# Moving the normed activations 64 bytes down in on-chip memory, in a five-layer fp32 transformer kernel

## The reference

```
h = layer_norm(ALPHA * h + mix, ln_g[i, 0], ln_b[i, 0])
h = layer_norm(ALPHA * h + square(relu(h @ w1)) @ w2, ln_g[i, 1], ln_b[i, 1])
```

```
x = x + 0.5 * (silu(n(x) @ w1) * (n(x) @ w3)) @ w2      # n: rmsnorm with a gain
x = x + hybrid_mixer(n(x), ...)
x = x + 0.5 * (silu(n(x) @ w1) * (n(x) @ w3)) @ w2
return n(x)
```

## Time and profile before

| | before |
|---|---|
| time, median of 3 runs | 2042.54 us (2042.12 to 2045.98) |
| time of the profiled execution | 2042.28 us |
| span of the profiled execution, first to last instruction | 2040.5 us |
| TensorE matmul busy | 1995.2 us, 98% of the span |
| TensorE weight loads busy | 1764.5 us, 86% |
| VectorE busy | 1321.0 us, 65% |
| ScalarE busy | 918.5 us, 45% |
| mean granted TensorE clock | 0.999 of full |

### The profile page before, as it was taken

One profiled execution on the slowest core, in us unless ns is written; L12 is line 12 of the kernel. 1 busy time (PEld: TensorE's weight loads), 2 busy tenths in 40 slices (PEclk: granted clock), 3 DMA queues, 4 the chain that ended last, 5 costly groups with the idle time before them and its releaser, 6 DMA issues.

```text
span 2040.5 us, 28917 instructions
## 1 busy us (share of the span) xinstructions
PE 1995.2 (98%) x12302; PEld 1764.5 (86%) x12302; DVE 1321.0 (65%) x1312; ACT 918.5 (45%) x860; POOL 22.5 (1%) x45
## 2 busy tenths in 40 slices
PE   8999999999999999999999999999999999999998
PEld 7988888797888888888988888889998997998997
DVE  6665866798756768667756666674445446666444
ACT  5345333367343554333344443443335445644444
POOL 0000000000000000000000000000000000000000
PEclk9999999999999999999999999999999999999999
DMA  8444555545545434555535455535556553344442
GB/s 335 167 158 173 186 181 189 186 150 186 217 175 206 143 147 186 189 185 185 204 124 206 160 202 205 179 121 188 188 201 218 168 142 124 124 165 155 185 185 103
DMA packets 31989, 361.72 MB, mean 177 GB/s; under 512 B 3805, under 2 KB 4066, under 8 KB 9746
## 3 DMA queue, kind: packets, MB, share of 16 engines
q1 hardware_dynamic: 28146, 347.49, 46.1%
q0 software_dynamic: 3744, 12.77, 2.6%
HBM read 359.15 MB, written 1.10 MB: 177 GB/s over the span
## 4 chain that ended last, share of the span: by engine, by line
PE 86%; DVE 8%; ACT 4%; issue 1%; DMA 0%; SPq 0%; DVEq 0%; ACTq 0%
PE acc L935 25%; PE bank L1541 9%; PE bank L825 8%; PE bank L827 8%; PE bank L826 7%; PE bank L1543 4%; DVE w_lo L2528 2%; PE bank L1554 1%; PE bank L864 1%; PE acc L947 1%; PE bank L866 1%; PE bank L865 1%; ACT w_hi L1938 1%; PE bank L1170 1%; PE bank L1658 1%
## 5 line engine op out<-in xcount | busy, mean ns | idle before, releaser
L2533 DVE TENSOR_TENSOR w_lo<-raw,w_hi 128x4096 fp32r<-128x4096 f32 (+4 forms) x83 | 310.2, 3737 | 117.3 <-ACT w_hi L1949 117.3
L825 PE MATMUL bank<-ht_both,w_hi 128*128 128x256 f32 x1344 | 376.8, 280 | 0.3 <-DVE oa_lo L3134 0.3
L827 PE MATMUL bank<-ht_both,w_lo 128*128 128x256 f32 x1344 | 375.5, 279 | 0.0
L826 PE MATMUL bank<-ht_both,w_hi 128*128 128x256 f32 x1344 | 375.0, 279 | 0.0
L1938 ACT ACTIVATE w_hi<-raw 128x2048 fp32r<-128x2048 f32 x166 | 309.6, 1910 | 136.2 <-PE bank L827 117.9
L1949 ACT ACTIVATE w_hi<-raw 128x4096 fp32r<-128x4096 f32 (+4 forms) x91 | 283.5, 3116 | 178.6 <-PE bank L1543 156.7
L2528 DVE TENSOR_TENSOR w_lo<-raw,w_hi 128x2048 fp32r<-128x2048 f32 x98 | 220.0, 2287 | 88.5 <-ACT w_hi L1938 88.5
L1541 PE MATMUL bank<-ht_both,w_hi 128*128 128x512 f32 x768 | 269.1, 393 | 0.0
L825 PEld LDWEIGHTS bank<-ht_both,w_hi 128*128 128x128 f32 x1344 | 251.9, 187 | 3.2 <-issue 1.3
L826 PEld LDWEIGHTS bank<-ht_both,w_hi 128*128 128x128 f32 x1344 | 252.3, 188 | 1.5 <-issue 0.5
L827 PEld LDWEIGHTS bank<-ht_both,w_lo 128*128 128x128 f32 x1344 | 252.2, 188 | 0.0
(11 more groups left out here) (470 smaller groups left out, 3355.5 us busy)
## 6 DMA issues: line engine op xcount, KB each, us to landing
raw<-slabs_in SPq DMA_DIRECT2D x147, 2048.0 KB, 7.8
raw<-slabs_in SPq DMA_DIRECT2D x23, 1024.0 KB, 6.9
raw<-slabs_in SPq DMA_DIRECT2D x12, 512.0 KB, 11.0
g_tab<-gains_in POOLq DMA_DIRECT2D x11, 512.0 KB, 4.4
b_tab<-gains_in POOLq DMA_DIRECT2D x8, 512.0 KB, 5.1
raw<-slabs_in SPq DMA_DIRECT2D x2, 1152.0 KB, 5.7
raw<-slabs_in SPq DMA_DIRECT2D x1, 1280.0 KB, 6.0
a_bias<-bias_rows POOLq DMA_DIRECT2D x8, 128.5 KB, 3.4
```

The source lines that it names most:

```text
L825: nc.tensor.matmul(o, whi, xhi, start=first, stop=False)
L826: nc.tensor.matmul(o, whi, xlo, start=False, stop=False)
L827: return nc.tensor.matmul(o, wlo, xhi, start=False, stop=last)
L2533: nc.vector.tensor_tensor(w_lo[ring][:, 0:w], raw[ring][:, 0:w], w_hi[slot][:, 0:w].bitcast(F32), ALU.subtract).then_inc(lo_ready, 1)
```

## The change

`ht_both` starts 64 bytes lower, at the weight slots' own remainder (0 instead of 64), and the bytes left free stand behind it, so that `cst` and all that follows stay where they were. The list of instructions is the same on every engine, in the same order and with the same waits; only the start addresses within `ht_both` differ.

```
         h = sb("h", [P, TT, D])
-        off_w(64)
         ht_both = sb("ht_both", [P, KD, 2, S], F32R)
         ht_hi = ht_both[:, :, 0, :]
         ht_lo = ht_both[:, :, 1, :]
-        off_w(192)
+        off_w(256)
         cst = sb("cst", [P, C_KEEP])
```

## The result

| | before | changed |
|---|---|---|
| median in the comparison | 2044.26 us (4 runs) | 2054.39 us (4 runs) |
| ratio to before | | 1.0050, 95% interval 1.0037 to 1.0062 |
| profiled execution | 2042.28 us | 2054.16 us |
| its span | 2040.5 us | 2052.4 us |

The forecast was 2050.5 us, slower, with a range of 2034 to 2078. The difference is clear of noise.

What follows compares the result with a forecast made beforehand. The prediction took PE's stream of matmuls, their number by the step, as the bound. Its terms, -4.1 - 2.2 + 14.7 - 0.5 = +7.9 us, gave 2050.2 us on the profiled execution, stated as 2050.5, range 2034 to 2078.

Steps and rivals of the forecast that it cites:

- The bound: Whole kernel: one long stream of matmuls on PE, its time the number of matmuls by the step between starts.
- Group 1: `ht_both` stationary, 512 weight columns moving, 624 matmuls: step falls from 233.3 to 226.7 ns, -4.1 us.
- Group 3: `ht_both` moving, 256 columns, 6,368 matmuls: step rises to 120.0 ns, +14.7 us.
- Group 2: `ht_both` moving, 512 columns, 896 matmuls on L1541 and L1554: step falls from 229.2 to 226.7 ns, -2.2 us.
- The sum: Whole kernel: -4.1 - 2.2 + 14.7 - 0.5 = +7.9 us, 2050.2 us on the profiled execution.
- The cover: Stages where VectorE ends the chain, as in RG-LRU: a few hundred slower matmuls are hidden, some 0.5 us.
- Rival A: 256-wide step does not depend on the remainder difference, only 512-wide matmuls gain: 2036.0 us; chance 0.20.
- Rival B: 256-wide matmuls at equal remainders fall into the 113.3 ns rhythm and stay: 2009 to 2025 us; chance 0.14.
- Rival C: 256-wide step rises to 122.5 to 126.6 ns at equal remainders: 2067 to 2094 us; chance 0.18.
- Rival D: The step depends on something other than remainders, which are a coincidence: 2042.5 us, same; chance 0.11.

Runs made afterwards that it cites:

- ht192: Kernel before with `ht_both` moved to remainder 192; 2032.45 us, ratio 0.9929.
- The grouped kernels: Changed kernel, kernel before and ht192, each with a bank's eight L1541 run before its eight L1543, not in turn; 2052.39, 2043.71 and 2027.95 us.
- w64: Kernel before with all weight slots and h 64 bytes higher, `ht_both` unmoved, so their remainders are equal; 2056.51 us, ratio 1.0051.
- group192: ht192 with the MLP's eight L1541 of a bank run first, then its eight L1543, instead of in turn; 2027.95 us, ratio 0.9925 to the kernel before.

## Why the prediction was right

**The bound.** Right. PE is the chain, its waits stayed, and the sum of the steps explains 11.8 of 11.9 us.

**Group 1, `tokens`.** Right in sign and in the settled step (226.7 ns). The 624 brought -2.6 us, not -4.1: the first turns of each run are slower until the streams settle, and L1730 got slower (a median of 233 after 229). The prediction left out the 192 matmuls of L1733 and L1734; they brought another -0.3.

**Group 3, 256 columns.** The step taken, 120.0 ns, is what came out wherever such matmuls run by themselves, and the stretches in the faster rhythm were lost, 240 matmuls taking 1.9 us more (1.6 forecast). The group brought +10.6 us where +14.7 was forecast; 3.1 of the difference is L1543, which in turn with L1541 became faster by 1.5 us and not slower by 1.6. The value was found by subtracting 106.7 ns from the 512-wide step at the same d. That derivation does not hold: by it d = 64 would be at 122.2, and d = 192, where ht192 measured 113.3, at 126.6. The likeliest value was right by a rule that fails at the other two, and that is luck. What the rows did bear out is the sign: the slow first matmuls at equal remainders pointed the right way. Its reason, that a 256-wide matmul has no quiet half without a load in which to settle, was tested by no run, and equal remainders are not special: d = 128 is as slow (120.0, 118.7).

**Group 2, 512 columns of `ht_both`.** Wrong in sign: -2.2 forecast for L1541 and L1554, +4.2 measured. L1554 went down by 0.3, L1541 up by 4.4. What failed is taking the settled step at d = 0 for them: that step is one of an uninterrupted run of like matmuls, and L1541 alternates with L1543. The grouped kernels show it.

**The sum.** On the profiled execution it is 2054.2 us against 2050.2. Group 2 came out 6.4 us above its term and group 1 1.5 above, group 3 4.1 below; the rest is 0.2. So the sign and the 256-wide step, which carry most of the sum, are the prediction's merit; that the sum is off by no more than 4 us is in part that its errors cancel.

**The cover.** The 0.5 us for stages that VectorE bounds were not separated by any run.

**Rival A** fell with group 3, and its ground fell too: `lu` at 192 does not stand for `up` at 192. **Rival B**, the 113.3 ns rhythm in `up`, is real, but mostly at d = 192, now and then at 64, and never at 0. **Rival C** was too high: 120.0 is the highest settled 256-wide step of `ht_both` at any d tried. **Rival D** is out by w64, where the difference changed without the buffer; of its case for two rhythms at one d something is left, since more than the remainders decides between them.

The prediction quoted a rule of the Trainium skill (page "TensorE: Matmul & The Clock Gate", section "Step-by-step: what each phase is for"), of two independent read ports and a weight load that takes no read bandwidth from the running matmul, and read it so that remainders would not matter. Read so, it does not hold here: the step at one shape goes from 226.7 to 234.3 ns and from 113.3 to 120.0 with them. Whether the ports are the reason no run shows.

**Open.** Why 32 or 64 bytes make a difference, what the two rhythms are inside the chip, and what beside remainders selects one in the stretches where kernels with equal remainders differ. That the operand's remainder acts on `up` through the down projections ahead of it is the likely reading, but other engines write the same operands while `up` runs, and no run separates the two. Whether the rhythm also goes by the number of matmuls ahead was not tried. The period of 256 bytes rests on one pair, 64 and 320.

## What to carry to other kernels

When matmuls run back to back, each with its own weight load, read the step from the timeline for every kind of matmul and set it beside the difference of the two operands' addresses modulo 256; here the best and the worst place of one buffer are 1.1% apart (2032.5 and 2054.4 us). Do it for each width and mix of widths apart, since 512 and 256 moving columns did best at different ones, and what is moved for one stage may cost in the stage behind it: measure the neighbours' steps, not only the time. Do not take a step from one short run or one trace, nor from a run of like matmuls for a mixed one.

## What was not expected of the hardware

- With 256 columns moving, a 192-byte difference gives 113.3 ns a matmul in most stretches (117.8 in the others) and 160 or 224 give 117.3 to 118.7: a change of 32 bytes costs 3 to 5%.
- The same instructions at the same addresses have two stable steps, 113.3 and 117.8 ns, each held for up to 480 matmuls on end (ht192, group192); in the feed-forward a neighbouring stage's operand address selects between them (16.40 against 16.75 us a block, 18 blocks of 18).
- A 512-wide and a 256-wide matmul in turn cost 353.1 ns a pair at d = 0, and 348.1 when grouped by eight (349.1 and 346.6 at d = 64), though the two kinds alone step at 226.7 and 120.0, together 346.7.
